# Four row loads go from the head of SP's load queue to the head of ScalarE's

## The chip, the cores and the metric

The kernel runs on one core of a Trainium2 chip. The time is the device time of one execution in microseconds, given as the median of several runs; 0.2% of it, 2.8 us, is about what a measurement of this kernel can tell from no change.

A core has five engines with an instruction queue each: TensorE (PE in the profile: matrix products; PEld is its loading of stationary operands), VectorE (DVE), ScalarE (ACT), GpSimd (POOL) and SyncE (SP), which here does nothing but issue loads. An engine runs its queue in order and waits at semaphores. SP, ScalarE and GpSimd can issue DMAs; the profile marks such an issue with SPq or ACTq. What the DMAs of SP move appears in the profile as queue q1, what those of ScalarE move as q10. Both are carried out by the same sixteen DMA engines.

## The reference

The kernel is a two-layer transformer encoder on 256 tokens of width 1024. Each layer gets its shifts, scales and gates ("modulation") from a vector c:

```python
c_act = jax.nn.silu(c)
for layer in range(DEPTH):
    mod = c_act @ ada_w[layer] + ada_b[layer]
    sh_m, sc_m, g_m, sh_f, sc_f, g_f = [t[:, None, :] for t in jnp.split(mod, N_MOD, axis=-1)]
    h = rms_norm(x, norm_mix_g[layer]) * (1.0 + sc_m) + sh_m
    x = x + g_m * token_mixer(h, cos, sin, w_in[layer], w_out[layer], ...)
    h = rms_norm(x, norm_ffn_g[layer]) * (1.0 + sc_f) + sh_f
    y = swiglu(h, ...) if layer % 2 == 0 else moe_swiglu(h, ...)   # 8 experts, top 2
    x = x + g_f * y
return rms_norm(x, final_g)
```

The change touches only the loads with which the first layer begins: c, two norm gains and a piece of the modulation bias ("the four rows", 4 to 8 KB each), x (1 MB), the token positions and rotary frequencies, and the first pieces of ada_w and w_in.

## The kernel before

All weights, some 475 MB, come from HBM once, through buffers in SBUF. SP's program is one long list of loads in the order in which the weights are used. Where a buffer has been used before, SP first waits until it is free; everything behind that load in its queue waits too.

The start of layer 0 is written out by hand, and this is what the change touches:

- SP (`row_loads`, L834) issues the four rows into the tile `vecrows`, then two modulation chunks of 2 MB each (`lead_ada(0)`, `lead_ada(1)`; the issue stands at L695), then two halves of the first w_in chunk, 1 MB each (`lead_columns_in`, L709). The third modulation chunk waits until TensorE has used the first; the next w_in half waits until the high and low parts of the first half are made; the fourth modulation chunk stands behind that half in the queue.
- ScalarE issues x (two loads, L924), the positions and the frequencies (L926), and then waits for the four rows. It applies silu to c (L928), then squares x with a running sum, once per 128 tokens (L947). Later it computes three sine tables (L1175 to L1177) and makes the high parts of the w_in halves (L991) and of the activations.
- VectorE's queue begins with two copies: the transposed rows (L1313) and c replicated for the matmuls, `c_rep` (L1314). Then it waits for x. Behind that stand, in this order: the mean squares (L1384), two normalisations of x into `xn` (L1391, with a power by GpSimd in between), some twenty small instructions for the sines' arguments (L1272 to L1286), the negated sines (L1308), and only then the first copy of a modulation row into `modrow` (L1327), `lead_round(0)`. Behind it are the second such round, the shifted and scaled activations `tmp` (L1355) and the low part of the first w_in half (L1259).
- TensorE waits for silu, transposes the rows (L2649), waits for `c_rep` and for the first modulation chunk, and multiplies it (`lead_chunk(0)`, 64 matmuls at L2117). It then transposes the 16 blocks of `xn` (L2161), then the block `modrow` (`lead_columns(0)`, L2127), and then multiplies the second chunk. After that it works on the projection with w_in, with the third and fourth modulation chunks in between.

Every weight of the first two projections is split into a high and a low part, so that three passes of TensorE (L2170 to L2172) give nearly full precision. Behind layer 0's attention and dense block follow layer 1 and its experts, whose weights (some 350 MB) stream through nine buffers; SP waits for TensorE there to give the buffers back (L766, L780).

The semaphore of the row loads, `rows_loaded`, is waited for by ScalarE alone; that of x, `x_loaded`, by ScalarE and VectorE.

Of the kernel before, what the change touches and what calls it, by code (L numbers as in the profile page):

```python
# [323 lines left out]
def build(nc, x_in, c_in, positions, inv_freq, ada_w, ada_b, mix_g, ffn_g, w_in, w_out, sink,  # L324
# [3 lines left out]
    with ExitStack() as ctx:  # L328
# [177 lines left out]
        def sem(name):  # L506
            return ctx.enter_context(nc.semaphore(name))
# [3 lines left out]
        rows_loaded, x_loaded = sem("rows_loaded"), sem("x_loaded")  # L511
# [44 lines left out]
        def bias_loads(layer, rounds):  # L556
# [4 lines left out]
        row_loads = [  # L561
            (vecrows[0:KD, :], c_in[0].rearrange("(k p) -> k p", p=P)),
            (vecrows[KD:3 * KD, :], mix_g.rearrange("l (k p) -> (l k) p", p=P)),
            (vecrows[3 * KD:5 * KD, :], ffn_g.rearrange("l (k p) -> (l k) p", p=P)),
            (vecrows[5 * KD:VECS, :], ada_b[0, 0:2 * D].rearrange("(k p) -> k p", p=P)),
        ]
# [111 lines left out]
        def _(sp):  # L678
# [33 lines left out]
            def lead_ada(n):  # L712
                s, a = LEAD[n]
                at = a * D + 512 * s
                load(("ada", 0, n), W[:, n % 2, :].rearrange("p (k n) -> p k n", k=KD),
                     ada_first[:, :, at:at + 512])
# [101 lines left out]
            def experts():  # L818
                expert = {0: N_EXP - 1}
                for kind, s, n, i in chunk_order()[EARLY:]:  # L820
                    if (kind, s, n, i) == ("gu", LAST, 0, 0):
                        overflow()
                    if s not in expert:
                        sp.wait_ge(table_ready, 1)
                        r = SLOT_RANK[s]
                        expert[s] = sp.value_load(table[0:1, 0, r:r + 1], min_val=0, max_val=N_EXP - 1)
                    g, b, _, prior = CHUNK_PLAN[(kind, s, n, i)]
                    if prior is None:
                        first_free(b)
                    else:  # L830
                        sp.wait_ge(main.used, prior + 1)
                    load_chunk(MainSlot(s), main, expert[s], kind, n, i)

            for dst, src in row_loads:  # L834
                sp.dma_start(dst, src).then_inc(rows_loaded, 16)
            lead_ada(0)
            lead_ada(1)
            lead_columns_in(0, 0)
# [81 lines left out]
        @block.scalar  # L920
        def _(act):

            for t in range(NT):
                act.dma_start(x[:, t, :], x_in[0, t * P:t * P + P, :]).then_inc(x_loaded, 16)  # L924
            for dst, src in step_loads:
# [1155 lines left out]
        def _(pe):  # L2081
            def ada_chunk(layer, n, bank=2):

                slot, _, loaded = plan[("ada", layer, n)]
                r, q = n // 4, n % 4
                pe.wait_ge(w_loaded[slot], loaded)
                if q == 0 and layer + r:
                    pe.wait_ge(mod_ready, 3 * layer + r)
                for kk in range(2):
                    k = 2 * q + kk  # L2090
                    for g in range(4):
                        mm = pe.matmul(ps[32 * g:32 * g + 32, bank, :], c_rep[:, k, :],  # L2092
                                       held(slot)[:, kk * 2048 + g * 512:kk * 2048 + g * 512 + 512],
                                       start=(k == 0), stop=(k == KD - 1))
                mm.then_inc(ada_used, 1)
# [10 lines left out]
            def lead_chunk(n):  # L2106

                s, a = LEAD[n]
                slot, _, loaded = plan[("ada", 0, n)]
                pe.wait_ge(w_loaded[slot], loaded)  # L2110
                if s and a:
                    pe.wait_ge(tr_copied, 2)
                rows = lead_block(n)[0]
                for kk in range(KD):
                    for g in range(4):
                        at = kk * 512 + g * P
                        mm = pe.matmul(rows[32 * g:32 * g + 32, :], c_rep[:, kk, :], W[:, slot, at:at + P],  # L2117
                                       start=(kk == 0), stop=(kk == KD - 1))
                mm.then_inc(ada_used, 1)
# [27 lines left out]
            def mod_columns(n):  # L2147

                pe.wait_ge(mod_ready, (1, 3, 4, 6)[n])
                for _, r, bank in COLUMN_ROUNDS[n]:  # L2150
                    for i in range(4):
                        mm = pe.transpose(ps[:, bank, i * P:i * P + P], modrow[:, r, i * P:i * P + P], ident[:])
                mm.then_inc(cols_ps, 1)
# [595 lines left out]
```

## Time and profile before

| | |
|---|---|
| median of 3 runs | 1408.1 us (1407.9 to 1409.03) |
| the profiled execution | 1409.18 us |
| its span | 1407.4 us |
| TensorE busy | 1299.9 us, 92% of the span |
| VectorE, ScalarE, GpSimd busy | 418.3, 291.1, 32.5 us |
| read from HBM | 477.32 MB, 340 GB/s over the span |

The span is the stretch between the first and the last instruction that the profile saw; the device time has some 1.8 us more around it. In the rows below an instruction has its start in microseconds from the span's beginning, its duration, its engine and its line in the kernel; "a<-b" is the tile that it writes and the one that it reads; brackets at the end tell how long the engine stood idle before it and what released it. For a DMA there are two different things: the issue on an engine's queue, some 0.4 us long, and the landing, when all its bytes are there. "DMA share" is the mean busy share of the sixteen DMA engines; it can come out a little above 1.

### The profile page before, as it was taken

Reading aid. Unit: us, or ns where it says so; the run is one execution under the profiler, and the core shown is the slowest. Engines: PE = TensorE matmul, PEld = TensorE weight load, DVE = VectorE, ACT = ScalarE, POOL = GpSimd, SP = SyncE. Lnnn points to the kernel's source line nnn. Section 1 sums busy time; section 2 is a strip of 40 time slices with the busy share of each in tenths; the row PEclk is TensorE's granted clock in tenths of the full one; section 3 lists DMA queues with packets and bytes.
Section 4 is the critical chain, followed back from the end, with each engine's and each line's share of the span. In section 5 each row is a group of like instructions: output and inputs, shape, how many; then the busy total and the mean of one; then the engine's idle time right before and its main releaser. Section 6 shows DMA issues by size and latency. Waiting matters only on the chain.

```text
span 1407.4 us, 24343 instructions
## 1 busy us (share of the span) xinstructions
PE 1299.9 (92%) x10618; PEld 691.8 (49%) x10619; DVE 418.3 (30%) x793; ACT 291.1 (21%) x528; POOL 32.5 (2%) x82
## 2 busy tenths in 40 slices
PE   5999999999999999999999999999689998997976
PEld 4766888888778576242333334333134332324221
DVE  4876854444468664200200000300001200001001
ACT  3336533343333552010000001000001000001001
POOL 1002000000000020000000000000000000000000
PEclk9999999999999999999999999999899999999999
DMA  9989665544575799999999999999999999999996
GB/s 333 323 342 326 208 212 195 190 179 179 212 265 209 319 362 368 401 405 409 408 352 404 365 398 409 409 408 408 409 395 408 409 409 409 409 392 403 408 404 246
DMA packets 146005, 481.98 MB, mean 342 GB/s; under 512 B 9032, under 2 KB 11152, under 8 KB 140784
## 3 DMA queue, kind: packets, MB, share of 16 engines
q1 hardware_dynamic: 141952, 475.06, 87.0%
q10 hardware_dynamic: 2720, 2.93, 0.8%
q0 software_dynamic: 1232, 2.50, 0.7%
q8 instruction: 80, 1.31, 0.4%
q14 instruction: 21, 0.17, 0.0%
HBM read 477.32 MB, written 1.05 MB: 340 GB/s over the span
## 4 chain that ended last, share of the span: by engine, by line
PE 65%; SPq 21%; DMA 5%; DVE 5%; ACT 2%; issue 2%; POOL 0%; DVEq 0%; POOLq 0%
PE ps L2482 21%; SPq L766 13%; PE ps L2532 10%; PE ps L2170 8%; PE ps L2172 8%; PE ps L2171 8%; SPq L780 6%; DMA raw<-in_moe_w_down_dram 3%; DMA weights<-in_ada_w_dram 2%; PE ps L2547 2%; PE ps L2092 2%; DVE weights_lo L1259 1%; PE ps L2251 1%; PE ps L2501 1%; PE ps L2224 1%
## 5 line engine op out<-in xcount | busy, mean ns | idle before, releaser
L2482 PE MATMUL ps<-raw,hX 128*32 128x512 f32 (+1 forms) x4416 | 479.2, 588 | 44.4 <-DMA raw<-in_moe_w_up_dram 26.3
L2482 PEld LDWEIGHTS ps<-raw,hX 128*32 128x32 f32 x4416 | 141.8, 111 | 350.3 <-issue 304.4
L2532 PE MATMUL ps<-raw,m_actT 128*32 128x512 f32 x1568 | 174.2, 593 | 15.3 <-DMA raw<-in_moe_w_down_dram 15.2
L2170 PE MATMUL ps<-weights_hi,hT_hi 128*128 128x512 f32 (+1 forms) x416 | 162.1, 390 | 2.7 <-DVE hT_lo L1362 1.4
L2172 PE MATMUL ps<-weights_hi,hT_lo 128*128 128x512 f32 (+1 forms) x416 | 159.0, 382 | 0.0
L2171 PE MATMUL ps<-weights_lo,hT_hi 128*128 128x512 f32 (+1 forms) x416 | 158.7, 381 | 0.0
L1656 DVE TENSOR_TENSOR m_actX<-m_sgX,ps 128x256 f32<-128x256 f32 (+1 forms) x20 | 7.7, 387 | 413.6 <-ACT m_sg L1110 277.8
L2532 PEld LDWEIGHTS ps<-raw,m_actT 128*32 128x32 f32 x1568 | 54.7, 110 | 128.5 <-issue 118.6
L1259 DVE TENSOR_TENSOR weights_lo<-weights,weights_hi 128x2048 fp32r<-128x2048 f32 (+1 forms) x52 | 113.2, 2204 | 2.3 <-ACT weights_hi L935 1.1
L935 ACT ACTIVATE weights_hi<-weights 128x2048 fp32r<-128x2048 f32 (+1 forms) x48 | 87.2, 1839 | 55.7 <-PE ps L2172 51.4
L1659 DVE TENSOR_TENSOR m_act<-m_sg,ps 128x512 f32<-128x512 f32 (+2 forms) x20 | 16.1, 805 | 260.2 <-ACT m_sg L1110 260.2
L2170 PEld LDWEIGHTS ps<-weights_hi,hT_hi 128*128 128x128 f32 x416 | 78.2, 188 | 21.1 <-issue 4.9
L2172 PEld LDWEIGHTS ps<-weights_hi,hT_lo 128*128 128x128 f32 x416 | 78.2, 188 | 15.5
L2171 PEld LDWEIGHTS ps<-weights_lo,hT_hi 128*128 128x128 f32 x416 | 78.4, 188 | 14.1
L2532 PE MATMUL ps<-raw,m_actTX 128*32 128x256 f32 x1120 | 67.5, 386 | 5.8 <-DMA raw<-in_moe_w_down_dram 5.4
L1108 ACT ACTIVATE m_sgX<-ps 128x256 f32<-128x256 f32 (+1 forms) x20 | 7.3, 364 | 292.5 <-PE ps L2482 292.5
L2532 PEld LDWEIGHTS ps<-raw,m_actTX 128*32 128x32 f32 x1120 | 38.6, 112 | 39.1 <-issue 14.9
L1110 ACT ACTIVATE m_sg<-ps 128x512 f32<-128x512 f32 (+2 forms) x20 | 13.8, 691 | 205.8 <-PE ps L2482 205.8
L1118 ACT ACTIVATE m_actTX<-ps 128x256 f32<-128x256 f32 (+1 forms) x20 | 7.1, 357 | 185.7 <-PE ps L2501 185.7
L2170 PE MATMUL ps<-down_hi,actT_hi 128*128 128x512 f32 x112 | 44.6, 399 | 0.0
L2172 PE MATMUL ps<-down_hi,actT_lo 128*128 128x512 f32 x112 | 43.7, 390 | 0.0
L2171 PE MATMUL ps<-down_lo,actT_hi 128*128 128x512 f32 x112 | 43.7, 390 | 0.0
(276 smaller groups left out, 1051.3 us busy)
## 6 DMA issues: line engine op xcount, KB each, us to landing
raw<-in_moe_w_gate_dram SPq DMA_DIRECT2D x112, 1024.0 KB, 16.8
raw<-in_moe_w_up_dram SPq DMA_DIRECT2D x112, 1024.0 KB, 18.4
raw<-in_moe_w_down_dram SPq DMA_DIRECT2D x110, 1024.0 KB, 16.7
weights<-in_ada_w_dram SPq DMA_DIRECT2D x18, 2048.0 KB, 9.8
weights<-in_ffn_w_gate_dram SPq DMA_DIRECT2D x14, 1024.0 KB, 5.6
weights<-in_ffn_w_up_dram SPq DMA_DIRECT2D x14, 1024.0 KB, 8.7
weights<-in_ffn_w_down_dram SPq DMA_DIRECT2D x7, 2048.0 KB, 9.8
weights<-in_w_in_dram SPq DMA_DIRECT2D x6, 2048.0 KB, 12.6
```

The lines of the kernel that those rows point to most:

```text
L766: sp.dma_start(dst[:, :, g, :], src.rearrange("a p k n -> p (a k) n")).then_inc(sig.loaded[b], 16)
L780: sp.dma_start(dst[:, 2 * h:2 * h + 2, :], src.rearrange("a p j n -> p (a j) n")).then_inc(sig.loaded[b], 16)
L935: act.activation(halves(hslot)[0][:, off:off + n], W[:, wslot, off:off + n], ACT.Copy).then_inc(hi_done, 1)
L1259: dve.tensor_tensor(lo[:, at], W[:, wslot, at], hi[:, at].bitcast(F32), ALU.subtract).then_inc(lo_done, 1)
L1659: i = dve.tensor_tensor(at[0], at[1], pair_banks[:, 0:a, 0:b, HU:2 * HU], ALU.mult)
L2092: mm = pe.matmul(ps[32 * g:32 * g + 32, bank, :], c_rep[:, k, :], held(slot)[:, kk * 2048 + g * 512:kk * 2048 + g * 512 + 512], start=(k = ...
L2170: pe.matmul(dst, stat_hi, hi, start=start, stop=False, skip_group_check=True)
L2171: pe.matmul(dst, stat_hi, lo, start=False, stop=False, skip_group_check=True)
L2172: return pe.matmul(dst, stat_lo, hi, start=False, stop=stop, skip_group_check=True)
L2482: mm = pe.matmul(ps[32 * q:32 * q + 32, bank, 0:2 * w].rearrange("p (g n) -> p g n", g=2), hX[:, k, at32:at32 + 32], weights[:, kk, :, at: ...
L2532: mm = pe.matmul(ps[32 * quarter:32 * quarter + 32, bank, col:col + w], stationary[:, 32 * half:32 * half + 32], raw[buffer][:, D * j + w ...
L2547: return pe.matmul(ps[:, bank, HU * t:HU * t + HU], pickT[c][rows, t, :], y, start=start, stop=stop, skip_group_check=True)
```

## The change

The four row loads are no longer issued by SP. ScalarE issues them, ahead of everything else that it has; x, the positions and the frequencies stand behind them. SP's queue begins with the first modulation chunk. No wait, no tile and no arithmetic changes.

```diff
@@ SP's program @@
-            for dst, src in row_loads:
-                sp.dma_start(dst, src).then_inc(rows_loaded, 16)
             lead_ada(0)
             lead_ada(1)
             lead_columns_in(0, 0)
@@ ScalarE's program @@
 
+            for dst, src in row_loads:
+                act.dma_start(dst, src).then_inc(rows_loaded, 16)
             for t in range(NT):
                 act.dma_start(x[:, t, :], x_in[0, t * P:t * P + P, :]).then_inc(x_loaded, 16)
             for dst, src in step_loads:
```

SP's queue at the start of the program, before (two lines of set-up stand ahead; `weights` are the load buffers, `x2` is two in a row):

```order
L835 DMA vecrows<-in_c_dram 8x128
L835 DMA vecrows<-in_norm_mix_g_dram 16x128
L835 DMA vecrows<-in_norm_ffn_g_dram 16x128
L835 DMA vecrows<-in_ada_b_dram 16x128
L695 DMA weights<-in_ada_w_dram 128x8x512 x2
L709 DMA weights<-in_w_in_dram 128x2x1024 x2
L695 DMA weights<-in_ada_w_dram 128x8x512
```

and after:

```order
L695 DMA weights<-in_ada_w_dram 128x8x512 x2
L709 DMA weights<-in_w_in_dram 128x2x1024 x2
L695 DMA weights<-in_ada_w_dram 128x8x512
L709 DMA weights<-in_w_in_dram 128x2x1024
L695 DMA weights<-in_ada_w_dram 128x8x512
```

The first modulation chunk is SP's first load now, and nothing else in SP's queue has moved. ScalarE's queue at the same place, as the difference between the two:

```order
-L920 UNCONDITIONAL_BRANCH
+L918 UNCONDITIONAL_BRANCH
+L922 DMA vecrows<-in_c_dram 8x128
+L922 DMA vecrows<-in_norm_mix_g_dram 16x128
+L922 DMA vecrows<-in_norm_ffn_g_dram 16x128
+L922 DMA vecrows<-in_ada_b_dram 16x128
 L924 DMA x<-in_x_dram 128x1024 x2
 L926 DMA pos_i<-in_positions_dram 128x2x1
```

Four issues stand ahead of x. TensorE's, VectorE's and GpSimd's instructions are the same, in the same order.

## Rows read from the trace of the kernel before

**Rows 1.** The page, part 4: the chain by engine.

```profile
PE 65%; SPq 21%; DMA 5%; DVE 5%; ACT 2%; issue 2%; POOL 0%; DVEq 0%; POOLq 0%
```

**Rows 2.** Chain of waits, 0 to 120 us: start us, duration us, what.

```profile
2.56 11.93 DMA weights<-in_ada_w_dram
14.63 3.64 PE ps L2117 x64
18.27 2.98 PE ps L2161 x16
...
28.35 11.34 DMA weights<-in_ada_w_dram
```

**Rows 3.** Timeline, issues of SP and ScalarE: start us, duration us, engine, line, operation.

```profile
0.79 0.41 SPq L835 DMA_DIRECT2D vecrows<-in_c_dram  x1
0.80 0.91 ACTq L924 DMA_DIRECT2D x<-in_x_dram  x2
...
2.10 0.42 SPq L835 DMA_DIRECT2D vecrows<-in_ada_b_dram  x1
2.22 0.49 ACTq L926 DMA_DIRECT2D inv<-in_inv_freq_dram  x1
...
2.56 1.33 SPq L695 DMA_DIRECT2D weights<-in_ada_w_dram  x2
```

**Rows 4.** Timeline, ScalarE and VectorE from 6 to 19 us.

```profile
6.81 0.31 ACT L928 ACTIVATE vecrows<-vecrows 8x128 f32<-8x128 f32 x1 [2.79 <-DMA vecrows<-in_ada_b_dram]
7.03 1.04 ACT L947 ACTIVATE xn<-x 128x1024 f32<-128x1024 f32 x1
...
7.87 0.29 DVE L1314 COPY c_rep<-vcols 128x256 f32<-128x256 f32 x1
...
10.49 0.75 DVE L1391 TENSOR_SCALAR xn<-x,rstd 128x1024 f32<-128x1024 f32 x1 [0.45 <-POOL rstd L889]
...
16.21 0.20 DVE L1308 TENSOR_SCALAR sinS<-sinS 128x64 f32<-128x64 f32 x1 [0.61 <-ACT sinS L1177]
...
18.39 0.29 DVE L1327 COPY modrow<-ps 128x128 f32<-128x128 f32 x1 [1.99 <-PE ps L2117]
```

**Rows 5.** Timeline from 20 to 28 us.

```profile
21.09 0.27 PE L2127 MATMUL ps<-ident,modrow 128*128 128x128 f32 x1
...
25.57 2.28 DVE L1259 TENSOR_TENSOR weights_lo<-weights,weights_hi 128x2048 fp32r<-128x2048 f32 x1
...
27.94 0.37 SPq L709 DMA_DIRECT2D weights<-in_w_in_dram  x1
```

**Rows 6.** Busy time by stretch: stretch, us, five engines, PEclk, DMA share, GB/s.

```profile
5.00:8.00 3.00, 0.32 (x1) 0.18 (x1) 0.34 (x2) 1.19 (x3) 0.00 (x0) 1.00 0.68 173
8.00:14.50 6.50, 0.00 (x0) 0.00 (x0) 4.70 (x20) 1.20 (x4) 1.54 (x2) 1.00 1.04 393
```

**Rows 7.** Landing times: L695 to 45 us; x; then L1191, its issues first.

```profile
DMA to landing us min/median/max: 11.3/12.4/16.9
...
DMA to landing us min/median/max: 3.9/4.3/4.8
...
L1191 ACTq DMA_DIRECT2D modrow<-in_ada_b_dram x4: 338/454/488, 57.3 to 58.7; - x4
...
DMA to landing us min/median/max: 5.9/6.4/7.3
```

**Rows 8.** DMA queues from 57.3 to 60.8, then from 60.8 to 62 us.

```profile
q1 hardware_dynamic: 696, 1.41, 105.7%
...
q1 hardware_dynamic: 131, 0.26, 67.1%
q10 hardware_dynamic: 77, 0.14, 39.5%
```

**Rows 9.** DMA queues from 0 to 5, then from 8 to 14.5 us.

```profile
q10 hardware_dynamic: 248, 0.95, 57.9%
...
q1 hardware_dynamic: 1262, 2.55, 103.4%
```

## The prediction

> **What bounds the kernel now.** I read the page first, then the chain of waits over the first 120 us, then the timeline of the first 60 us engine by engine, and last the DMA views of short stretches. The page says that the end is set by TensorE for 65% of the chain and by SP's queue, which waits for free buffers, for 21% [rows 1]. So nothing in the middle of the program stands still for a fixed time: each load is issued when a buffer is given back, and each matmul group starts when a load or an operand is there. An edit that touches only the first 4 us is worth what it moves the first link of that chain, as long as every later link depends on the one before.
>
> The first links are in [rows 2]. The chain begins with the transfer of the first modulation chunk (2 MB), issued at 2.56 us and landed at 14.6. Then TensorE multiplies it (64 matmuls, 3.64 us), transposes the 16 blocks of the normalised x (2.98 us), and at 21.09 transposes the modulation row that VectorE copied [rows 5]. From there it goes over the second chunk and VectorE to the buffer of the first w_in half: its low part ends at 25.57 + 2.28 = 27.85, SP issues the next w_in half at 27.94 [rows 5] and the fourth modulation chunk at 28.35 [rows 2]. All that follows hangs on these two issues. What has to be found is by how much the transpose at 21.09 moves, because the part up to it has two inputs: the chunk, and VectorE's copy of the modulation row.
>
> **The change part by part.** On SP four issues go away from the head: they start at 0.79 and the last ends at 2.52 [rows 3]. The first chunk is issued at 0.79 instead of 2.56, which is 1.77 us earlier. The second chunk and the two w_in halves behind it move with it.
>
> What does the transfer make of these 1.77 us? Between 5 and 8 us the DMA engines moved 173 GB/s, between 8 and 14.5 us 393 GB/s [rows 6]. That is the hole between the end of x and the moment at which the weights run at full rate: 3 x (393 - 173) / 393 = 1.68 us of full rate lost. With the chunk queued from 0.79 on, x and chunk overlap, their bytes are the same, and the hole has nothing that would make it. I take 1.7 us: the chunk lands at 14.6 - 1.7 = 12.9. The bounds: nothing (the hole is the slow start of the first weight reads and only moves), and 2.5 us (the 1.7 plus some 0.8 from a narrower spread of the sixteen engines, for which the distance of 16.9 to 11.3 us between landings of the same 2 MB load speaks [rows 7]).
>
> TensorE's side is then 12.9 + (21.09 - 14.63) = 19.36 us for the transpose, if nothing else is late.
>
> On ScalarE four issues come to the head. Each takes some 0.4 us (the four on SP took 1.73 together), so x, positions and frequencies, issued from 0.80 to 2.71 before [rows 3], are issued some 1.65 us later: x at about 2.45 and 2.9. ScalarE's table load behind them comes later by the same and is hidden, since silu waits for the rows anyway.
>
> The four rows: the last was issued at 2.10 and silu started at 6.81, so it took 4.7 us at most [rows 3, 4]. In the changed kernel it is issued at about the same time, but behind weights instead of ahead of them. For such a small load on ScalarE's queue behind a busy SP queue the trace has one case, the four bias loads at 57.34: 5.9 to 7.3 us to landing [rows 7]. So the rows land between 2.1 + 4.7 = 6.8 and 2.1 + 7.3 = 9.4. From there to the end of the replicated c, 7.87 + 0.29, which the first matmuls need, it was 8.16 - 6.81 = 1.35 us [rows 4], so it is there at 8.2 to 10.8. The chunk at 12.9 hides it. If that cover went, each us of delay past 12.9 would be one us of the result.
>
> x is the dear part. Before, x was no limit: it landed 3.9 and 4.8 us after its issue, by 6.1 at the latest [rows 7], and ScalarE began the squares at 7.03 because silu stood ahead [rows 4]. Now x is issued later and has company. In the bias case no packet of ScalarE's queue moved for 3.5 us after the issue, while SP's queue moved 696; then in 1.2 us SP's moved 131 and ScalarE's 77 [rows 8]. So I let x start 3.5 us after 2.45, at about 5.95, and give it every second packet. Its packets are of 4 KB (248 for 0.95 MB), the weights' of 2 KB (1262 for 2.55 MB) [rows 9]: x gets two thirds of 393 GB/s and its 1.05 MB take 4.0 us. It lands at 10.0. The bounds are 7.7 (2.9 + 4.8, as undisturbed as before) and 16 (all that SP has queued, 6.3 MB at 393 GB/s, goes ahead). I take 10.0 because the bias loads are the nearest rows to it.
>
> Behind x stands VectorE's whole queue up to the copy of the modulation row: mean squares, two normalisations, the sine arguments, the negated sines. It ended at 16.21 + 0.20 = 16.41 and the copy came at 18.39, when TensorE was done [rows 4]: 1.98 us of idle time. Squares at 10.0 instead of 7.03 put its end at 16.41 + 3.0 = 19.4, the copy's end at 19.7 and the transpose at 19.75. That is later than TensorE's own 19.36, so the last input changes from the chunk to VectorE. The gain at this point is 21.09 - 19.75 = 1.3 us. The normalised x itself, ready at 10.49 + 0.75 = 11.24 before [rows 4], is ready at about 14.2, ahead of its first transpose at 12.9 + 3.64 = 16.5. Positions and frequencies are first needed at 14.2; they are issued 2 us after x and are small.
>
> Behind it the shift goes through. The low part at 25.57 shows no idle time ahead of it [rows 5], so VectorE had come from other work and not from a wait for the first w_in half; that load moves by the same 1.7 us and stays hidden. SP's issues at 27.94 and 28.35 come 1.3 us earlier. No later stage starts by the clock on the wall, so I let the 1.3 us stand to the end.
>
> The sum, against the profiled execution: 1409.18 - 1.3 = 1407.9 us (span 1407.4 - 1.3 = 1406.1). The median of the runs is 1.1 us lower than that execution, so I predict 1408.1 - 1.3 = 1406.8.
>
> **A rule that speaks against it.** The Trainium skill, page "DMA: Bandwidth & Descriptors", section "Queues, rings and completion order", says that each DMA engine goes round its queues by packets of some 9 to 17 descriptors, at most 64, and not one by one. The trace leans against large turns, since 77 packets of one queue came beside 131 of the other in 1.2 us, that is 5 beside 8 on each engine, but it can't show the order on a single engine. By the rule the sum would be that of the first rival.
>
> **The rivals.**
> Late x, in turns (slower). If an engine serves 16 weight packets for every load that it takes from ScalarE's queue, a turn is 16 x 16 x 2.0 KB / 393 GB/s = 1.3 us. Four rows and two x loads wait six turns, 7.9 us, and x's own bytes take 2.7 us at full rate; from a first packet at 1.8 that is 12.4. VectorE's chain then ends at 16.41 + 5.4 = 21.8 and the transpose comes at 22.15, 1.1 us later than before: 1409.2. It decides from x at 11.4 on (21.09 - 0.35 - 16.41 = 4.33 us after 7.03). In the extreme form, all that SP has queued goes ahead: x at 16 plus 2.7, less what overlaps, and the loss is some 8 us: 1416.
> The hole stays. If the low rate from 5 to 8 us is the first weight reads' own, whenever they start, the chunk lands at about 14.4. VectorE's 19.75 is then in time and the gain is 0.2: 1407.9. For it: SP's queue moved little even after x was through. Against: the weights were issued only at 2.56 and later, behind the rows and small loads, and the same queue ran at full rate from 8 us on.
> More than forecast. If SP's queue isn't deep yet when x is issued, x lands at about 8.6, VectorE is done at 18.0, and TensorE's side alone counts. With the engines closer together the chunk lands at 12.3 and the gain is 2.3: 1405.8.
>
> **How the numbers follow.** My forecast has a chance of 0.42, x in turns 0.15, its extreme 0.05, the hole that stays 0.20, more than forecast 0.15; 0.03 is for what I don't see. All but the extreme lie within 2.5 us of 1408.1, and 0.2%, what a measurement of this kernel can tell from no change, is 2.8 us. So "the same" takes 0.80; faster by more than that needs the upper bound of the landing, an early x and luck, 0.10; slower by more needs the extreme or a piece of the turns, 0.10. The range reaches from 1404.6 (a gain of 2.5 us and 1 us of scatter, as the runs of before show) to 1410.6 (the turns with the same scatter); it leaves out the extreme.
>
> **What would show it right or wrong.** The first chunk's issue at 0.8 us and the first TensorE matmul on it near 12.9; DMA rate between 5 and 8 us near 390 GB/s; silu between 7 and 9.5; squares of x near 10; the copy of the modulation row following VectorE's own chain and not TensorE; the transpose near 19.75; SP's issues at 26.6 and 27.0; the span near 1406. I am wrong if squares start past 11.4, if the chunk lands after 14, or if the issues near 27 are early and the end isn't.

## The result, and the profile after

| | before | after |
|---|---|---|
| median of 13 runs each | 1408.54 us (1407.9 to 1409.3) | 1411.67 us (1410.68 to 1412.26) |
| the profiled execution, its span | 1409.18, 1407.4 us | 1410.91, 1409.2 us |
| TensorE busy | 1299.9 us | 1303.5 us |

The ratio after to before is 1.0021, with a 95% interval from 1.0014 to 1.0028: slower by 3.1 us. That is clear of no change; against the 0.2% (2.8 us) at which a difference counts here it is on the edge, since the interval begins at 0.14%. The forecast was 1406.8, with a range up to 1410.6 and a chance of 0.10 on slower. It was wrong in sign and outside its range.

The load stream filled the hole, as was forecast. Busy time by stretch, against [rows 6] (the last two rows are of stretches further on):

```profile
5.00:8.00 3.00, 0.00 (x0) 0.00 (x0) 0.00 (x0) 1.46 (x2) 0.00 (x0) 1.00 1.05 401
8.00:14.50 6.50, 3.37 (x61) 3.26 (x65) 1.24 (x5) 2.19 (x4) 0.89 (x2) 1.00 1.00 356
...
17.00:21.40 4.40, 0.09 (x1) 0.00 (x0) 3.31 (x16) 1.07 (x4) 0.00 (x0) 1.00 1.02 409
21.40:25.40 4.00, 3.82 (x65) 3.11 (x65) 0.35 (x3) 1.27 (x1) 0.00 (x0) 0.57 1.06 393
```

The hole between 5 and 8 us is filled, 401 GB/s where there were 173. Part of it is given back between 8 and 14.5 us, 356 GB/s where there were 393: by 14.5 us the changed kernel has moved 4.4 MB and the kernel before 4.0. But the first link of the chain of waits is another one (start, duration, what; against [rows 2]):

```profile
3.25 8.44 DMA x<-in_x_dram
11.71 2.20 ACT xn L947 x4
...
21.93 3.42 PE ps L2117 x64
...
30.42 11.24 DMA weights<-in_ada_w_dram
```

The chain begins with x, not with the modulation chunk, and its fourth modulation chunk is issued at 30.42 where [rows 2] have 28.35. The timeline of the changed kernel, against [rows 3 to 5]:

```profile
2.77 1.03 ACTq L924 DMA_DIRECT2D x<-in_x_dram  x2
...
7.62 0.31 ACT L928 ACTIVATE vecrows<-vecrows 8x128 f32<-8x128 f32 x1 [1.48 <-DMA vecrows<-in_ada_b_dram]
...
8.69 0.29 DVE L1314 COPY c_rep<-vcols 128x256 f32<-128x256 f32 x1
...
11.45 3.53 PE L2117 MATMUL ps<-weights,c_rep 128*32 128x128 f32 x64 [3.05 <-DMA weights<-in_ada_w_dram]
11.71 1.06 ACT L947 ACTIVATE xn<-x 128x1024 f32<-128x1024 f32 x1 [3.77 <-DMA x<-in_x_dram]
...
20.91 0.20 DVE L1308 TENSOR_SCALAR sinS<-sinS 128x64 f32<-128x64 f32 x1 [0.61 <-ACT sinS L1177]
21.14 0.29 DVE L1327 COPY modrow<-ps 128x128 f32<-128x128 f32 x1
...
21.49 0.45 PE L2127 MATMUL ps<-ident,modrow 128*128 128x128 f32 x1 [4.40 <-DVE modrow L1327]
...
21.86 3.44 PE L2117 MATMUL ps<-weights,c_rep 128*32 128x128 f32 x64
...
30.01 0.37 SPq L709 DMA_DIRECT2D weights<-in_w_in_dram  x1
```

The same stretches and the same chunk in the kernel before:

```profile
17.00:21.40 4.40, 4.40 (x45) 3.85 (x41) 0.30 (x2) 0.00 (x0) 0.00 (x0) 1.00 1.04 409
21.40:25.40 4.00, 3.52 (x79) 3.25 (x78) 1.89 (x8) 1.91 (x1) 0.00 (x0) 1.00 1.03 391
...
21.29 1.95 PE L2117 MATMUL ps<-weights,c_rep 128*32 128x128 f32 x64
```

Read the brackets. The squares of x waited 3.77 us for x alone. The copy of the modulation row has no bracket: VectorE reached it late, out of its own work. The transpose of that row waited 4.40 us for the copy, and the chunk behind the transpose took 3.44 us. In before the same 64 matmuls took 1.95 us. The granted clock (the number behind the five engines) of 21.40 to 25.40 is 0.57 of full, against 1.00 in before: most of it went at the lower of TensorE's two levels, 1.2 instead of 2.4 GHz, after 4.40 us without a matmul. So the change costs twice: a later transpose, and a slower chunk behind it.

### The profile page after: what moved, and what is told of

Same layout as the page of the kernel before. It is cut to its first block, busy times and chain, and to the rows that moved or that the text cites. A ratio compares the mean times of both kernels' runs of the same rounds, so it can differ in the third digit from the quotient of the medians.

```text
span 1409.2 us, 24343 instructions
## 1 busy us (share of the span) xinstructions
PE 1303.5 (92%) x10618; PEld 693.6 (49%) x10619; DVE 418.1 (30%) x793; ACT 290.9 (21%) x528; POOL 32.4 (2%) x82
## 3 DMA queue, kind: packets, MB, share of 16 engines
q10 hardware_dynamic: 2832, 2.96, 0.7%
HBM read 477.32 MB, written 1.05 MB: 339 GB/s over the span
## 4 chain that ended last, share of the span: by engine, by line
PE 64%; SPq 18%; DMA 8%; DVE 5%; ACT 2%; issue 2%; ACTq 0%; POOL 0%; DVEq 0%; POOLq 0%
PE ps L2482 20%; SPq L766 11%; PE ps L2532 9%; PE ps L2170 8%; PE ps L2172 8%; PE ps L2171 8%; SPq L780 7%; DMA raw<-in_moe_w_down_dram 3%; DMA raw<-in_moe_w_up_dram 3%; PE ps L2547 2%; PE ps L2092 2%; DMA weights<-in_ada_w_dram 1%; DVE weights_lo L1259 1%; PE ps L2452 1%; PE ps L2251 1%
## 5 line engine op out<-in xcount | busy, mean ns | idle before, releaser
L2532 PE MATMUL ps<-raw,m_actT 128*32 128x512 f32 x1568 | 177.5, 602 | 15.6 <-DMA raw<-in_moe_w_down_dram 15.4
```

The source lines that it names most:

```text
L2532: mm = pe.matmul(ps[32 * quarter:32 * quarter + 32, bank, col:col + w], stationary[:, 32 * half:32 * half + 32], raw[buffer][:, D * j + w ...
```

## The experiments

Each kernel ran in five rounds beside the kernel before, 11 runs each, and only 6 of the one with the sines out of the way; medians of the kernel before were 1408.51 to 1408.60 us. "SP at 27" is the start of SP's issue of the third w_in half, 27.94 us in the profile shown ahead of the prediction. "Ratio" is the time against the kernel before, with its 95% interval.

**The two ends again.** The same two kernels were run once more, to learn how much of the 3.1 us, and of the 27.94, belongs to one execution.

> The kernel before itself, measured in the place of a changed kernel, because eight variants so far gave a median about 0.6 to 1.3 us higher than the shift of SP's issue near 28 us in their profiles says. Theory (the first profile of the kernel before was an ordinary one, and the extra is scatter of single profiles): 1408.5 within 0.4, ratio 1.0000, SP's issue at 27.9 and a span near 1407. Rival (that profile was a slow sample at its start): SP's issue comes at 27.3 or earlier in this one.

Measured: 1408.43 us (1407.79 to 1409.41), ratio 0.9999 [0.9990, 1.0008]. The timeline of this execution of the kernel before:

```profile
14.99 3.64 PE L2117 MATMUL ps<-weights,c_rep 128*32 128x128 f32 x64 [7.53 <-DMA weights<-in_ada_w_dram]
...
18.57 2.02 PE L2161 MATMUL ps<-ident,xn 128*128 128x128 f32 x16
...
20.43 0.27 PE L2127 MATMUL ps<-ident,modrow 128*128 128x128 f32 x1
...
27.28 0.37 SPq L709 DMA_DIRECT2D weights<-in_w_in_dram  x1
```

The transposes of `xn` took 2.02 us here and 2.98 in [rows 2]. The first profile was 0.66 us later at this point than this one: its chunk left 0.36 us earlier, and its transposes took 1.0 us more. So the rival of the expectation held, SP's issue at 27.3 or earlier. The time of this execution, 1408.57 us, is nearer to the median than the 1409.18 of the first, and the distances below are taken from its 20.43 and 27.28. It is one execution too: in the thirteen profiles of this document these 16 transposes took 2.0 to 3.0 us, so that a single distance can be off by up to 1 us.

> The changed kernel once more, beside the other three on one chip, to measure them against it. Theory: 1411.7 within 0.5, 3.1 us over the kernel before. Of these 3.1 us the profiles showed 2.1 at SP's issue of 30.0 and 1.8 at the end. Rival (the median of the first measurement lay high): 2 us over the kernel before.

Measured: 1411.47 us (1410.53 to 1412.64), ratio 1.0021 [1.0012, 1.0030]. Transpose at 21.52, second chunk 3.11 us, clock 0.63 from 21.4 to 25.4, SP at 29.74. The loss is the kernel's, 3.0 us this time.

**Keep TensorE busy while it waits.**

```diff
+            keep(18, 2)      # 36 matmuls of ident into a free bank
             lead_columns(0)
             lead_chunk(1)
```

> The changed kernel with 36 idle matmuls on TensorE (four bytes wide of meaning: they only multiply the identity into a bank that nothing reads) between its transposes of x and the transpose that waits for VectorE's copy. They fill the 4.4 us in which TensorE stood still in the changed kernel. Theory (x is late, and the standstill that this makes costs once more, because TensorE's granted clock falls to the lower level in the next chunk): the transpose stays at 21.5 us, the second chunk takes 1.95 us instead of 3.4, SP's issues of 30.0 and 30.4 come at about 28.5 and 28.9, and the time is 1.5 us under the changed kernel's 1411.7, so 1410.2. Rival (the chunk was slow for another reason, such as its own late landing or contention): the chunk takes 3.4 us still and the time is 1411.7.

Measured: 1410.19 us (1409.40 to 1410.61), ratio 1.0010 [1.0001, 1.0019].

```profile
16.87 4.18 PE L2100 MATMUL ps<-ident 128*128 128x128 f32 x36
...
21.41 0.33 PE L2127 MATMUL ps<-ident,modrow 128*128 128x128 f32 x1 [0.36 <-DVE modrow L1327]
21.68 1.96 PE L2117 MATMUL ps<-weights,c_rep 128*32 128x128 f32 x64
...
28.33 0.37 SPq L709 DMA_DIRECT2D weights<-in_w_in_dram  x1
```

Nothing useful was added, the transpose is where it was (21.41), and the chunk behind it takes 1.96 us again, at a granted clock of 1.00. SP is 1.68 us earlier than in the changed kernel and the median 1.5 us lower, as expected; the slowest of these runs, 1410.61 us, is about as fast as the fastest ones of the changed kernel (1410.68, and 1410.53 when it was run again). About half of the loss is the clock. The edit takes away nothing but the idle time ahead of the chunk, so the price is that of the standstill and not of the chunk's own landing. The Trainium skill, page "TensorE: Matmul & The Clock Gate", section "HAM oscillation — how this bites in real kernels", says that a wait for data between bursts of matmuls lets the chip take the clock back, and that the next burst starts slow. By that rule the trace agrees: 0.57 behind the wait of 4.40 us, 1.00 with the wait filled.

**x ahead of the rows.** ScalarE issues x first and the rows behind it.

```diff
+            for t in range(NT):
+                act.dma_start(x[:, t, :], ...)
             for dst, src in row_loads:
                 act.dma_start(dst, src)
-            for t in range(NT):
-                act.dma_start(x[:, t, :], ...)
```

> The changed kernel with x ahead of the four rows on ScalarE's queue. SP still begins with the modulation chunk. Theory (what costs is x's place behind the weights' first packets): x is issued at 0.8 us, lands by 7, the rows land by 8.5, the squares start at about 8.5 instead of 11.7, VectorE's chain ends at 17.9, the transpose comes at 18.0 to 18.3 with the second chunk at full clock, SP's issues near 30 come at 25.2, and the time is 3 us under the kernel before: 1405.5. Rival (SP's early chunk holds everything of ScalarE's queue back, whatever stands first): x lands no earlier than 10, and the time stays over 1410.

Measured: 1407.56 us (1407.15 to 1408.28), ratio 0.9992 [0.9983, 1.0001].

```profile
9.43 0.31 ACT L928 ACTIVATE vecrows<-vecrows 8x128 f32<-8x128 f32 x1 [3.39 <-DMA vecrows<-in_ada_b_dram]
9.64 1.04 ACT L947 ACTIVATE xn<-x 128x1024 f32<-128x1024 f32 x1
...
12.59 3.64 PE L2117 MATMUL ps<-weights,c_rep 128*32 128x128 f32 x64 [2.38 <-DMA weights<-in_ada_w_dram]
...
19.40 0.33 PE L2127 MATMUL ps<-ident,modrow 128*128 128x128 f32 x1 [1.13 <-DVE modrow L1327]
19.66 1.96 PE L2117 MATMUL ps<-weights,c_rep 128*32 128x128 f32 x64
...
26.31 0.37 SPq L709 DMA_DIRECT2D weights<-in_w_in_dram  x1
```

4.1 us against the changed kernel, from the order of ScalarE's first six issues alone. x is no longer what ends last: the squares have no bracket, they stand behind silu, and silu waits for the rows. The wait of TensorE for the copy is 1.13 us, and the chunk behind it takes 1.96 us. The time is 2 us above what I expected. I had the rows at 8.5 and silu came at 9.43, and I had put no price on the chunk: it leaves at 12.59 instead of 11.45. From 2 to 4 us SP's queue moved 0.12 MB here and 0.50 MB in the changed kernel; the rest of the rate went to x.

**The rows on GpSimd's queue.** x is ScalarE's first issue, the rows are GpSimd's first.

```diff
-            for dst, src in row_loads:
-                act.dma_start(dst, src)
 @@ GpSimd's program @@
+            for dst, src in row_loads:
+                pool.dma_start(dst, src)
             pool.memset(ident[:], 0.0)
```

> The changed kernel with the four rows on GpSimd's queue, at its head; ScalarE's queue begins with x. Theory: x is issued at 0.8 and lands by 7; the rows, four issues of some 0.6 us and 5.5 us to landing as GpSimd's loads at 43 to 45 us had, land at about 8.5; the rest as with x first: transpose near 18.3, time 1405.5 to 1406. Rival (the rows are what holds ScalarE back then): rows at 10 or later, squares behind them, VectorE's chain at 19.5 or later, and the time is 1407 or more.

Measured: 1407.40 us (1406.70 to 1408.10), ratio 0.9993 [0.9984, 1.0002]. Silu at 9.09, squares 9.30, chunk 12.57, transpose 19.07, SP 25.98. Within noise of the version above, and over the 1405.5 to 1406 that I expected: the rows came 0.6 us later than I had them and the transpose 0.8.

**What makes x late: its own issue or SP's queue ahead of it?** Here SP first issues four loads of the same size and source as before, into a tile that nobody reads, and the rest is the changed kernel. x is still ScalarE's fifth issue, at 2.74, but the weights behind SP's head are issued at 2.56 again instead of 0.79.

```diff
+            for dst, src in idle_row_loads:       # same sources, other tile
+                sp.dma_start(dst, src)
             lead_ada(0)
```

> The changed kernel with four small loads put back at the head of SP's queue: they bring the same rows into a tile that nobody reads, and only hold SP's first chunk back to 2.56 us, where it was before. ScalarE's queue is that of the changed kernel, so x is still issued at 2.8. Theory (x was late because the weights' packets had filled the DMA engines' queues for 2 us before it was issued, and not because its own issue came 2 us later): x starts within 1.5 us of its issue and lands by 9.5, the squares start by 9.5, VectorE's chain ends by 18.9, the transpose is again TensorE's own at 20.5 to 21.1, the second chunk takes 1.95 us, and the time is that of the kernel before, 1408.5 within 0.6. Rival (x's own late issue and its sharing are enough): x lands at 11 or later and the time is over 1410.5.

Measured: 1408.90 us (1408.55 to 1409.43), ratio 1.0002 [0.9993, 1.0011].

```profile
2.74 0.93 ACTq L929 DMA_DIRECT2D x<-in_x_dram  x2
...
10.34 1.06 ACT L952 ACTIVATE xn<-x 128x1024 f32<-128x1024 f32 x1 [3.75 <-DMA x<-in_x_dram]
...
14.23 3.64 PE L2122 MATMUL ps<-weights,c_rep 128*32 128x128 f32 x64 [7.17 <-DMA weights<-in_ada_w_dram]
```

The squares were expected by 9.5 and came at 10.34, so I missed their place; the time was right. Of the 4.7 us by which the squares are later than in before (7.03 to 11.71), 1.4 are the weights that got ahead of x. The other 3.3 are x's later issue and its sharing with the weights, together; no run here separates the two. The traces give a split of x's landing, from 6.05 in before to 11.69 in the changed kernel: the issue is 2.0 us later, the first bytes come about 1 us after it in before (between 1.5 and 2.0) and about 4 in the changed kernel (between 6.5 and 6.8), and the bytes themselves take about 0.7 us longer.

**The sines out of the way.** VectorE copies the modulation row first and does the sine work behind the last part of the projection's lead.

```diff
-            steps(); negative_sines()
             lead_round(0)
             lead_round(1)
 ...
             low_of("in", 0, 1, 1)
+            steps(); negative_sines()
```

> The changed kernel with the sine work (VectorE's arguments, ScalarE's three tables, the negated sines) moved behind the last part of the lead projection, so that VectorE's copy of the first modulation row stands right behind the normalisation of x. x lands as late as in the changed kernel. Theory (x's lateness costs only through the 5 us of VectorE's work between it and the copy): the copy comes at about 16, the transpose at 17.1, the second chunk starts with its landing at about 18.3 at full clock, SP's issues near 30 come at 25 to 25.5; the sine work costs up to 1 us later, where VectorE is busy for 47 of 56 us: 1405.5 to 1407. Rival (x's or the rows' lateness costs elsewhere, in the transposes of x or in the projection): the issues near 30 stay later than 27.9 and the time over 1408.5.

Measured: 1413.14 us (1412.73 to 1414.21), ratio 1.0032 [1.0020, 1.0045], the slowest of all. The place came out as expected: transpose at 17.55, second chunk 1.96 us, SP at 24.65, 5.4 us earlier than in the changed kernel. The time did not:

```profile
52.10 0.26 ACT L1183 ACTIVATE cosF<-arg 128x64 f32<-128x64 f32 x1 [6.71 <-DVE arg L1286]
...
54.55 4.50 DVE L1259 TENSOR_TENSOR weights_lo<-weights,weights_hi 128x2048 fp32r<-128x2048 f32 x2 [1.68 <-ACT weights_hi L935]
...
59.12 0.37 SPq L695 DMA_DIRECT2D weights<-in_w_out_dram  x1
```

ScalarE waits 6.71 us for the sines' arguments, the high and low parts behind them are late, and SP issues the w_out load at 59.12, where before it was at 54.59. The expectation had 1 us for this and 1407 at most. What had cost VectorE 5 us under a transfer now costs it 5 us at its busiest. So the run shows the sine work to be what stands between x and the transpose, and shows no gain from it.

**Only the first copy ahead of the sines.**

```diff
+            lead_round(0)
             steps()
             negative_sines()
-            lead_round(0)
             lead_round(1)
```

> The changed kernel with VectorE's first modulation round (the copy that the transpose waits for) ahead of the sine work, which stays ahead of the second round. x lands as late as in the changed kernel. Theory (x's lateness costs through the place of this copy behind the sine work, and the standstill costs the clock): the copy comes at 15.9, the transpose at 17.5, the second chunk at 17.8 takes 1.95 us at the higher clock; the sine work runs from 18.4 to 23.7 and the second round's copy comes at 23.7 (23.4 before, 25.5 in the changed kernel). The time is 1.7 us under the changed kernel's: 1410.0. Rival (the copy's place isn't what costs): second round's copy at 25.4 and no gain over 1411.7.

Measured: 1409.78 us (1408.63 to 1411.03), ratio 1.0007 [0.9998, 1.0016]. Right. The second chunk starts at 17.96 and takes 1.95 us, and then TensorE stands for the second copy instead:

```profile
24.10 0.48 PE L2127 MATMUL ps<-ident,modrow 128*128 128x128 f32 x1 [4.18 <-DVE modrow L1327]
...
24.37 5.57 PE L2100 MATMUL ps<-ident 128*128 128x128 f32 x36
28.47 0.37 SPq L709 DMA_DIRECT2D weights<-in_w_in_dram  x1
```

The standstill only moved, and the clock with it: the 36 filler matmuls behind it take 5.57 us instead of the 4.18 that they took in the changed kernel. (The kernel has this burst of its own, behind the second transpose of a modulation row.) The granted clock from 24.3 to 30.0 us is 0.74.

**Three attempts at a better start**, on a version above. First, on the version with x ahead: squares ahead of silu, and VectorE's work on x ahead of its two copies.

```diff
-            columns()
             dve.wait_ge(x_loaded, 16 * NT)
             mean_square(0, 0); mean_square(0, 1)
             normal(0, 0); normal(0, 1)
+            columns()
```

> The kernel with x first on ScalarE's queue, and in addition everything that works on x stands ahead of what works on the rows: ScalarE squares x before silu, VectorE makes the means and the normalised x before it copies the transposed rows. Theory (with x first, the rows were what VectorE's chain waited for: silu at 9.4 with x there by 6.9): squares at 7, normalised x at 11.1, replicated c at 11.7, still ahead of the chunk at 12.5, VectorE's chain ends at 16.9, the transpose is TensorE's own at 18.4 instead of 19.4, and the time is 1 us under that kernel's 1407.6: 1406.5. Rival (the chain is set by positions and frequencies, which are last on the queue): the sine work waits for them until 12.5 or later and the time is 1407.3 or more.

Measured: 1407.88 us (1406.94 to 1408.49), ratio 0.9994 [0.9985, 1.0003]. Squares at 8.75, which is where x landed, later than I had it. Silu then comes at 12.25 only, and the first matmul waits for `c_rep` until 13.66: what x won the rows gave back. Of silu's delay 1.28 us are ScalarE's table load, which stands between squares and silu here (at 10.95 us) and elsewhere runs while ScalarE waits for the rows. I had expected 1406.5.

Second and third, the positions and frequencies on GpSimd's queue and the sines' arguments at VectorE's head: on the changed kernel, and on the version with x ahead.

```diff
+            steps()                      # third: ahead of columns()
             dve.wait_ge(x_loaded, 16 * NT)
 ...
-            steps()
-            negative_sines()
             lead_round(0)
+            negative_sines()
```

> The changed kernel, with rows ahead of x on ScalarE's queue as it is, and the sine work moved into the 4 us in which VectorE waited for x: positions and frequencies are loaded by GpSimd at the head of its queue, the sine arguments stand right behind the replicated c and ahead of x, the negated sines behind the first round's copy. Theory (x's late landing costs only by what stands behind it on VectorE): positions and frequencies there by 7.5, sine arguments from 9.0 to 14.1, normalised x at 16.5, the copy at 16.7, the transpose at 17.8 with no standstill over 1 us on TensorE, the second chunk at full clock, SP's issue near 25: 3 us earlier than before, and the time 1406 within 0.8. Rival (x's late landing itself is the limit): the transpose at 19 or later, 1408 or more.

> The same idea on the kernel with x first on ScalarE's queue and the rows behind: positions and frequencies by GpSimd, the sine arguments ahead of the transposed rows on VectorE. Theory: sine arguments from 7.5 to 12.6, replicated c at 13.2 (0.7 us behind the chunk's landing at 12.5), first chunk's matmuls at 13.2, transpose at 19.2, SP's issue at 26 and a time of 1407.4: no better than x first alone, and worse than the rows-first version, because the chunk shares the first microseconds with x. Rival (x early is worth more than the chunk early): under 1406.

Measured: 1408.06 us (1407.15 to 1410.39), ratio 0.9998 [0.9989, 1.0007], and 1409.48 us (1407.53 to 1410.40), ratio 1.0004 [0.9995, 1.0013]. I had expected 1406 and 1407.4. In the second, silu starts at 9.80 and the squares at 13.55, where the changed kernel has 7.62 and 11.71. The two small loads on the third queue did not only go ahead: from 6 to 7 us all queues together moved 0.14 MB, where the changed kernel moved 0.41. Even so its time is about 3.5 us below that of the changed kernel, with x 1.8 us later: the transpose came at 18.87, since the sine work was done before x was there, and between the first two chunks TensorE waited 1.06 us at most. So it isn't x's landing that costs, but the landing and the work that stands behind it together. In the third VectorE's head waited for the frequencies until 9.77 and `c_rep` came at 14.37, so that the first matmul left at 14.71, 2 us after its chunk landed. Neither beats the plain reordering.

**The shift at SP against the time.** Distance from the kernel before (27.28 us and the job's own median), in us:

| kernel | SP at 27 | median |
|---|---|---|
| changed | +2.73 | +3.13 |
| changed, again | +2.46 | +2.96 |
| TensorE kept busy | +1.05 | +1.64 |
| first copy ahead | +1.19 | +1.27 |
| x ahead, arguments early | +0.66 | +0.88 |
| SP with four idle loads | -0.25 | +0.39 |
| x ahead | -0.97 | -0.99 |
| x work first | -1.22 | -0.63 |
| rows on GpSimd | -1.30 | -1.15 |
| arguments early | -1.55 | -0.54 |

What moves at 27 us arrives at the end, to within 1.0 us. The sines-late kernel isn't in the table: it changes work behind that point, and its SP is 2.6 us early and its end 4.6 late.

## Why the prediction was wrong, by its own steps

- **The first chunk's issue at 0.79: right**, and the hole of [rows 6] was real: 401 GB/s. The rival that the hole stays is out. The chunk's landing was mis-sized: forecast at 12.9 with a bound of 2.5 us on the gain, and its first matmul ran at 11.45, 3.2 us earlier than before. x and the chunk are 3.15 MB. In before 4.0 MB had moved by 14.5 us, in the changed kernel 3.5 MB by 11.5: 0.5 MB less of later loads had gone ahead of the chunk's last part, which at 393 GB/s is 1.3 us; with the hole's 1.7 that is 3.0 of the 3.2 us. The upper bound named such a spread between the engines, but read its size from rows that don't show it: the landing of 16.9 us in [rows 7] is that of the second chunk, which stands behind the first.
- **The rows, 6.8 to 9.4, hidden: right** (silu 7.62, `c_rep` done at 8.98, 2.5 us ahead of the chunk).
- **x lands at 10.0: the step that failed.** It landed by 11.69. The table shows where, in us:

| | forecast | measured |
|---|---|---|
| first issue | 2.45 | 2.77 |
| its bytes begin | 5.95 | 6.5 to 6.8 |
| its last bytes | 10.0 | about 10.9 |
| signal seen by ScalarE | 10.0 | 11.7 |

  The DMA queues of the changed kernel, from 7 to 8 us:

```profile
q10 hardware_dynamic: 66, 0.26, 67.1%
q1 hardware_dynamic: 66, 0.14, 36.2%
```

  x got every second packet and two thirds of the bytes, exactly as the working had it, and 4 us for them was right. Between 5 and 6 us ScalarE's queue had moved 0.01 MB and SP's 0.39. Wrong were the terms at both ends: the lag before the first bytes, up to 4.0 us instead of 3.5, an issue 0.3 us later than supposed, and 0.7 us between the last bytes and the signal, for which the sum had no term at all. The bound of 16 us was far too wide. The rival "in turns" had the time of x nearly right (12.4) for a reason that the trace refutes: 66 packets beside 66 aren't sixteen of the weights for each load of x. Nor are they equal turns: in each quarter of a microsecond from 7 to 10.5 us x's queue moved 16 to 22 packets and SP's 16 to 21. x is 256 packets, 16 for each engine, so in turns of 9 or more SP's queue would have stood nearly still for a time, and it never did. That answers the rule of the Trainium skill, page "DMA: Bandwidth & Descriptors", section "Queues, rings and completion order", which the prediction weighed: as the trace counts packets (2 KB of weights, 4 KB of x), the measurement decides against turns of 9 to 17.
- **VectorE's chain sets the transpose: right in form.** Its sum was the chain's 16.41 plus the lateness of the squares: 16.41 + (11.71 - 7.03) = 21.09, and 0.35 to the transpose gives 21.44. Measured: 21.49. Its own threshold, x at 11.4, was crossed by 0.3 us, and "squares past 11.4" was its first sign of being wrong. Positions and frequencies, which the working called small, landed at 13.3 and 14.7, behind the 14.2 at which it needed them; with x late VectorE came to them at 15.85, so they cost nothing.
- **Missing: the price of TensorE standing still, a term that the sum had at nothing.** With the squares at 10.0 the forecast itself left TensorE idle only shortly. But each microsecond that the chunk came early (1.5) and x late (1.7) widened the wait, to 4.40 us (most of the rest are the 16 transposes, 2.18 us here and 2.98 in [rows 2]), and nowhere did the working ask what such a wait costs beyond its length. It costs 1.2 to 1.5 us, shown by the filled wait and again by the wait that moved.
- **The base was off by 0.66 us, as far as two executions tell.** The first profile of before had slow transposes; the second has 20.43 where the working subtracts from 21.09. Even with x at 10.0 the gain would have been 20.43 - 19.75 = 0.7 and not 1.3.
- **The shift goes through to the end: right**, by the table.
- **The range** was given as the turns' 1409.2 with 1 us of scatter, which is 1410.2 and not 1410.6; 1411.67 is outside either.

The sum: 21.49 - 20.43 = 1.06 us of later transpose, and 3.44 or 3.11 instead of 1.95 us for the chunk, which is 1.2 to 1.5 more. That makes 2.2 to 2.6 of the 3.1 us measured, and SP's issue shows 2.46 and 2.73. The remaining 0.4 to 0.9 us lie within the scatter of single executions and stay open. That the clock is half of it is shown by experiment; that it all comes from x's place behind the rows is shown by the reordering, which takes all of it away and 1 us more.

Four versions have a median below the kernel before, by 0.5 to 1.15 us, and all four intervals reach 1.0. The best two are x ahead (0.07%) and the rows on GpSimd (0.08%). They are no proven gain; they show that the first modulation chunk at SP's head is harmless when nothing is put ahead of x.

## What to carry to other kernels

Moving small loads out of one queue puts them at the head of another: price the load behind them there, from its issue to the signal, since a megabyte issued 2 us later behind a filled queue came 5.6 us later here. An operand that gains an early arrival gains nothing if its partner is late, and a wait of TensorE can have a second price in the clock of the burst behind it, which belongs in the sum: waits of 4.2 to 4.4 us had it here, one of 1.13 us had not. And take the baseline of a step from two executions where a microsecond decides.

## What the runs showed of the hardware that was not expected

- x, issued on ScalarE's queue while SP's was full of weights, moved nothing for about 4 us, where alone it had begun after about 1. Then it went packet for packet: 66 beside 66 between 7 and 8 us, so that packets of 4 KB take two thirds from packets of 2 KB.
- The same 16 transposes took 2.02 us in one execution of the kernel before and 2.98 in another, with a granted clock of 1.00 in both rows. One by one (duration as minimum, median, maximum in ns), in the second execution and then in the first:

```profile
L2161 PE MATMUL ps<-ident,xn x16: 272/273/383, 18.6 to 20.3; 128*128 128x128 f32 x16
```

```profile
L2161 PE MATMUL ps<-ident,xn x16: 272/421/476, 18.2 to 21.0; 128*128 128x128 f32 x16
```

  And the first chunk takes 3.64 us in nine of the thirteen profiles and 3.18 to 3.57 in the others; the second, of the same form, takes 1.95 or 1.96 but where TensorE had stood still. The durations speak for the lower level after the idle start, the clock column of these rows says 1.00. It seems that the column can't be trusted before the first change of the clock that it records; no run here settles it. If it is so, the kernel before pays the slow clock once, and the changed one twice.
- Two small loads (17 KB) moved to GpSimd's queue made the rows, on another queue, 2.2 us later (silu 7.62 to 9.80), and with x ahead 1.2 us (9.43 to 10.62). Why so little data costs so much no run here shows.
